# Silu of a convolution branch as z times 1/(1+exp(-z)): exponential on ACT, sum, reciprocal and product on VectorE

## What is computed

```python
def conformer_branch(z, dw_w, dw_b, ln_g, ln_b):
    a, g = jnp.split(z, 2, axis=-1)
    u = a * jax.nn.sigmoid(g)
    u = depthwise_conv(u, dw_w) + dw_b
    u = layernorm(u, ln_g, ln_b)
    return jax.nn.silu(u)
...
    merged = jnp.concatenate([
        rmsnorm(attn, g_branch[:MLA_WIDTH]),
        rmsnorm(conf, g_branch[MLA_WIDTH:MLA_WIDTH + CONF_WIDTH]),
        rmsnorm(sc, g_branch[MLA_WIDTH + CONF_WIDTH:])], axis=-1)
    return merged @ w_o
```

## Time and profile before

| | us |
|---|---|
| median of 3 runs (1690.57, 1695.78, 1696.7) | 1695.78 |
| the profiled execution, whole | 1697.5 |
| its span, first to last instruction | 1695.6 |
| TensorE matmul busy | 1610.2 |
| VectorE busy | 1026.9 |
| ACT busy | 838.2 |
| GpSimd busy | 76.3 |
| mean granted TensorE clock | 0.983 |

### The profile page before, as it was taken

One profiled execution on the slowest core, in us unless ns is written; L12 is line 12 of the kernel. 1 busy time (PEld: TensorE's weight loads), 2 busy tenths in 40 slices (PEclk: granted clock), 3 DMA queues, 4 the chain that ended last, 5 costly groups with the idle time before them and its releaser, 6 DMA issues.

```text
span 1695.6 us, 25551 instructions
## 1 busy us (share of the span) xinstructions
PE 1610.2 (95%) x10226; PEld 1379.8 (81%) x10226; DVE 1026.9 (61%) x1616; ACT 838.2 (49%) x1484; POOL 76.3 (4%) x60
## 2 busy tenths in 40 slices
PE   7998999999999999999989999999999988889997
PEld 6887789998888999987557588888888874779996
DVE  6855865567686566779764643333333687565665
ACT  5434275553826566353574552415244455665554
POOL 1200300000030000000000000000000100010000
PEclk9999999999999999999999999999999998999999
DMA  8733765556756555533101532232322231135551
GB/s 302 267 117 129 258 228 183 186 177 222 273 174 224 177 185 185 198 137 109 41 1 63 211 102 98 94 102 90 99 93 82 75 137 38 63 125 174 186 186 49
DMA packets 69937, 247.49 MB, mean 146 GB/s; under 512 B 7504, under 2 KB 10576, under 8 KB 69712
## 3 DMA queue, kind: packets, MB, share of 16 engines
q1 hardware_dynamic: 69840, 246.18, 42.4%
HBM read 245.10 MB, written 1.05 MB: 145 GB/s over the span
## 4 chain that ended last, share of the span: by engine, by line
PE 75%; DVE 12%; issue 7%; ACT 4%; DMA 0%; POOL 0%; DVEq 0%; SPq 0%; ACTq 0%; POOLq 0%
PE psum L375 15%; PE psum L377 15%; PE psum L376 14%; PE psum L396 9%; PE psum L397 5%; DVE lo_ring L336 3%; PE psum L1142 2%; PE psum L1815 2%; PE psum L410 1%; DVE c_conf L2093 1%; PE psum L411 1%; PE psum L412 1%; PE psum L1838 1%; PE psum L1825 1%; PE psum L510 1%
## 5 line engine op out<-in xcount | busy, mean ns | idle before, releaser
L375 PE MATMUL psum<-x_parts,hi_ring 128*128 128x256 f32 (+1 forms) x1464 | 459.9, 314 | 14.2 <-DVE x_parts L901 11.7
L336 DVE TENSOR_TENSOR lo_ring<-raw_ring,hi_ring 128x1024 fp32r<-128x1024 f32 x348 | 432.2, 1243 | 62.7 <-PE psum L377 21.1
L376 PE MATMUL psum<-x_parts,hi_ring 128*128 128x256 f32 (+1 forms) x1464 | 455.4, 311 | 0.0
L377 PE MATMUL psum<-x_parts,lo_ring 128*128 128x256 f32 (+1 forms) x1464 | 455.4, 311 | 0.0
L348 ACT ACTIVATE hi_ring<-raw_ring 128x1024 fp32r<-128x1024 f32 x292 | 307.3, 1053 | 256.4 <-PE psum L377 137.7
L375 PEld LDWEIGHTS psum<-x_parts,hi_ring 128*128 128x128 f32 x1464 | 280.5, 192 | 36.0 <-issue 17.6
L376 PEld LDWEIGHTS psum<-x_parts,hi_ring 128*128 128x128 f32 x1464 | 280.6, 192 | 15.0 <-issue 0.2
L377 PEld LDWEIGHTS psum<-x_parts,lo_ring 128*128 128x128 f32 x1464 | 280.5, 192 | 14.7
L396 PE MATMUL psum<-hid_parts,hi_ring 128*128 128x512 f32 x672 | 235.2, 394 | 0.3 <-DVE lo_ring L336 0.3
L1420 DVE TENSOR_TENSOR hid_parts<-relu,hid_parts 128x256 fp32r<-128x256 f32 (+1 forms) x128 | 63.0, 493 | 221.1 <-ACT relu L1409 221.1
L397 PE MATMUL psum<-hid_parts,lo_ring 128*128 128x256 f32 x672 | 188.3, 280 | 0.0
(11 more groups left out here) (430 smaller groups left out, 2344.7 us busy)
## 6 DMA issues: line engine op xcount, KB each, us to landing
raw_ring<-weights SPq DMA_DIRECT2D x460, 512.0 KB, 3.4
h_const<-hyb_consts SPq DMA_DIRECT2D x1, 1088.0 KB, 11.3
x<-xT SPq DMA_DIRECT2D x1, 1024.0 KB, 8.2
x<-ctxT SPq DMA_DIRECT2D x1, 1024.0 KB, 16.7
outT<-x SPq DMA_DIRECT2D x4, 256.0 KB, 2.5
shared<-shared_consts SPq DMA_DIRECT2D x1, 398.0 KB, 13.4
par<-params SPq DMA_DIRECT2D x1, 301.5 KB, 8.2
```

Source lines behind the costliest of these rows:

```text
L336: nc.vector.tensor_tensor(lo_ring[:, s, :], raw_ring[:, UNIT_AT[u] % RAW_SLOTS, :], hi_ring[:, s, :].bitcast(F32), ALU.subtract).then_inc( ...
L375: nc.tensor.matmul(bank(u % BANKS, T), w_hi, hi[:, k, 0:T], start=(k == 0), stop=False)
L376: nc.tensor.matmul(bank(u % BANKS, T), w_hi, lo[:, k, 0:T], start=False, stop=False)
L377: last = nc.tensor.matmul(bank(u % BANKS, T), w_lo, hi[:, k, 0:T], start=False, stop=(k == KT - 1))
```

## The change

ACT no longer computes silu. VectorE applies gain and offset itself, ACT takes exp(-z) for both halves in one instruction (the attention's table has exp), VectorE adds one, takes the reciprocal and multiplies, and ACT squares the result in one instruction. One flag, conf_gate, counts the three handovers. The new VectorE step "gate" stands at turn 6 of layer 0 and turn 5 of layer 1. Some steps after it move by a turn. In the first-block and second-block MLP the flag half_added is replaced by VectorE's own step counter; the instructions between stay.

```diff
@@ mlp_dve
-                    nc.vector.tensor_tensor(y[:, j, 0:T], side_by_side(u)[:, 0], y[:, j, 0:T], ALU.add).then_inc(flag("half_added"), 1)
+                    nc.vector.tensor_tensor(y[:, j, 0:T], side_by_side(u)[:, 0], y[:, j, 0:T], ALU.add).then_inc(dve_step, 1)
+                    link.count += 1
                     next_lo(dve, u)
-                    now["half_added"] += 1
-                    dve.wait_ge(flag("half_added"), now["half_added"])
+                    dve.wait_ge(dve_step, link.count)
@@ tables
-    PE_STEPS = [{1: ["mean"], 3: ["sums"], 5: ["sc"], 7: ["again"]}, {0: ["mean"], 3: ["sums"], 4: ["sc"], 7: ["again"]}]
-    ACT_STEPS = [{2: ["squares"], 3: ["rstd"], 5: ["silu"], 6: ["sc_rstd"], 8: ["last"]},
-                 {2: ["squares"], 3: ["rstd"], 4: ["silu"], 6: ["sc_rstd"], 7: ["last"]}]
-    DVE_STEPS = [{1: ["center"], 4: ["scaled"], 8: ["sc"], 15: ["last"]}, {1: ["center"], 3: ["scaled"], 6: ["sc"], 8: ["last"]}]
+    PE_STEPS = [{1: ["mean"], 3: ["sums"], 5: ["sc"], 8: ["again"]}, {0: ["mean"], 3: ["sums"], 4: ["sc"], 7: ["again"]}]
+    ACT_STEPS = [{2: ["squares"], 3: ["rstd"], 5: ["exp_neg"], 6: ["sc_rstd"], 7: ["squares_again"], 9: ["last"]},
+                 {2: ["squares"], 3: ["rstd"], 4: ["exp_neg"], 6: ["squares_again", "sc_rstd"], 7: ["last"]}]
+    DVE_STEPS = [{1: ["center"], 4: ["scaled"], 6: ["gate"], 8: ["sc"], 15: ["last"]}, {1: ["center"], 3: ["scaled"], 5: ["gate"], 6: ["sc"], 8: ["last"]}]
@@ branch_act
-            if step == "silu":
-                for i in range(2):
-                    act.wait_ge(flag("conf_scaled"), 2 * l + i + 1)
-                    other_set()
-                    link(nc.scalar.activation(c_conf[:, i, 0:T], c_conf[:, i, 0:T], ACT.Silu, scale=pcol("conf_g", 2 * l + i),
-                                              bias=pcol("conf_beta", 2 * l + i)))
-                    last = nc.scalar.activation(c_sq[:, i, 0:T], c_conf[:, i, 0:T], ACT.Square)
-                last.then_inc(flag("conf_sq"), 1)
+            if step == "exp_neg":
+                act.wait_ge(flag("conf_gate"), 3 * l + 1)
+                exp_set()
+                nc.scalar.activation(c_sq[:, :, 0:T], c_conf[:, :, 0:T], ACT.Exp, scale=-1.0).then_inc(flag("conf_gate"), 1)
+            if step == "squares_again":
+                act.wait_ge(flag("conf_gate"), 3 * l + 3)
+                nc.scalar.activation(c_sq[:, :, 0:T], c_conf[:, :, 0:T], ACT.Square).then_inc(flag("conf_sq"), 1)
@@ branch_dve
             if step == "scaled":
                 dve.wait_ge(flag("branch_rstd"), 2 * l + 1)
+                link(nc.vector.tensor_tensor(c_conf[:, :, 0:T], c_conf[:, :, 0:T], bc(rstd[:, 0:T], 2), ALU.mult))
                 for i in range(2):
-                    nc.vector.tensor_tensor(c_conf[:, i, 0:T], c_conf[:, i, 0:T], rstd[:, 0:T], ALU.mult).then_inc(flag("conf_scaled"), 1)
+                    last = nc.vector.tensor_scalar(c_conf[:, i, 0:T], c_conf[:, i, 0:T], pcol("conf_g", 2 * l + i), pcol("conf_beta", 2 * l + i),
+                                                   ALU.mult, ALU.add)
+                last.then_inc(flag("conf_gate"), 1)
+            if step == "gate":
+                dve.wait_ge(flag("conf_gate"), 3 * l + 2)
+                link(nc.vector.tensor_scalar(c_sq[:, :, 0:T], c_sq[:, :, 0:T], 1.0, None, ALU.add))
+                link(nc.vector.reciprocal(c_sq[:, :, 0:T], c_sq[:, :, 0:T]))
+                nc.vector.tensor_tensor(c_conf[:, :, 0:T], c_conf[:, :, 0:T], c_sq[:, :, 0:T], ALU.mult).then_inc(flag("conf_gate"), 1)
```

More of the change, by code:

```diff
@@ L1394, in late_scaled_dve @@
         lo(KT - 1)
-    now["half_added"] = 0
     def mlp_act(act, link, m, base, T):
```

## The result

| | before | after |
|---|---|---|
| median of 14 runs each, us | 1695.14 | 1701.09 |
| lowest to highest | 1690.54 to 1698.74 | 1697.38 to 1704.15 |
| span of the profiled execution | 1695.6 | 1699.7 |

The ratio is 1.0034, with a 95% interval of 1.0024 to 1.0043: the change costs 5.8 us of 1695. The forecast was 1705.6 us in a range of 1698 to 1710: the sign and the places were right, the size was too large.

What follows compares the result with a forecast made beforehand. The prediction took TensorE, waiting for ACT's silu and table loads in the attention, to bound the kernel. Layer 0's +6.0 us and layer 1's +3.8 us made +9.8 us on the median 1695.78 us: 1705.6 us, range 1698 to 1710 us.

Steps and rivals of the forecast that it cites:

- What bounds: Both layers' attention: TensorE waits behind ACT's silu and table loads; after the change the chain goes through the gate.
- about 10 us: Silu step in both layers: the time of the whole kernel said to hang on it, about 10 us.
- The loads: ACT around silu: four table loads at 1.28 us, 5.1 us in all, against 10.6 us by the skill's figure.
- The reciprocal: VectorE's gate: 8.2 us in layer 0 and 4.15 us in layer 1, called what decides.
- the floor that I supposed: 2-column reciprocal row: may rest on a minimum time, putting the slope at 8.3 ns a column, 8.7 and 4.4 us.
- The clock: TensorE behind its wait for the gate: half clock adds 2.1 us in each layer.
- The rival without a loss: TensorE behind the gates: clock isn't lost or returns at once, +5.6 us, 1701.4 us; chance 0.11.
- "scaled" hidden: VectorE: about 1 us more in layer 0 and 0.6 in layer 1, covered because top(7) waits for TensorE anyway.
- Its own range: Whole kernel: +8.1 to +11.8 us, from the ends of reciprocal and clock.
- The counter: MLP: another counter round the same instructions costs nothing, unless the wait falls differently.
- The quick reciprocal: VectorE's gate: reciprocal at one column per cycle, sum -4.9 us, 1690.9 us; chance 0.10.
- "same": Whole kernel: outcome not told from no change, within about 0.5%, 8.5 us; chance 0.44.

Runs made afterwards that it cites:

- e8: The kernel before with silu replaced by the identity, so no table is loaded for it; 1687.4 us, ratio 0.9958.
- e6: The kernel before with 8 reciprocals and 8 additions of 2 to 1024 columns added behind VectorE's last work; one run, 1708.09 us.
- e5: The changed kernel with 7 useless matmuls in each of TensorE's two waits for the gate; 1698.64 us, ratio 1.0025.
- e7: The kernel before with only the MLP's counter exchanged for VectorE's own step counter; 1696.37 us, ratio 1.0017.
- e11: A repeat of e7, the kernel before with only the MLP's counter exchanged; 1694.87 us, ratio 1.0003.
- e1: The changed kernel with the reciprocal replaced by a minimum with 1.0 of the same shape; 1688.18 us, ratio 0.996.
- e2: The changed kernel with the reciprocal dropped and the sigmoid made on ACT as exp(-ln(1+exp(-z))), VectorE keeping the product; 1689.8 us, ratio 0.9969.
- e9: The e2 kernel with layer 0's three ACT instructions at turns 5, 6 and 7 and the steps around them moved; 1689.75 us, ratio 0.9978.
- e10: A repeat of e2, beside e9 on the same chip; 1690.63 us, ratio 0.9975.

## Why the prediction was right, and where its size was off

- **What bounds.** Right: the chain left ACT, as said, and went over the gate in both layers. e8 shows that the four loads, 5.1 us long, had cost 6.9. That "about 10 us" hang on the whole step wasn't tried: no run took silu's own work out too.
- **The loads.** 1.28 us each with the next instruction at once, and 1.41 us of ACT's time by e8. By the Trainium skill's 2.66 us a switch ("ScalarE: Activation LUTs", What ACT_TABLE_LOAD costs) e8 would have gained 10.6 us, an estimate from that page, and e8's interval ends at 9.7. Here the measurement decides against that figure as a cost on this path.
- **The reciprocal.** The deciding step named rightly, and mis-sized: I took 8.2 and 4.15 us, the rows have 6.55 and 3.35, below even my lower bound of 7.7 and 3.9. I drew a line through 2 and 8 columns and carried it to 1024. The 2-column reciprocal (160 ns in the earlier trace rows, 156 in e6) lies under the line of e6 (153 + 12.5 = 165), so the slope came out at 7.3 instead of 6.25; the floor that I supposed points the wrong way, for it isn't there. The Trainium skill's repeat count of 8 ("VectorE: DVE Perf Modes", First, the fixed hardware budget), read as 8 cycles a column, isn't what e6 shows: six. That is 1.65 us of layer 0's error and 0.8 of layer 1's.
- **The clock.** Taken at 2.1 us more in each layer; e5 shows 1.6 and 1.6. I had 4 to 5.4 us of work at half clock, but part of the low stretch fell into the wait, and TensorE worked only 3.3 us in it each time. The window of 1425 to 1430 us that I leaned on the earlier trace rows was misread: in before the clock is at 0.50 from about 1417.2 to 1430.8 us, from the end of an earlier wait of 2.62 us on, and not from the wait of 2.27 us at 1425 us. The rival without a loss is out: both windows behind the gates are at 0.50. In layer 0 before had paid for its own fall as well, which the sum had in it.
- **"scaled" hidden.** True in layer 0. In layer 1, out_pair(2) waits 0.30 us for pair_out(1) behind it (the row at 1444.17 us above), and top(7) comes 0.37 us later than in before. I had looked at top(7) alone and not at pair_out(1), which stands next in VectorE's stream.
- **The sum by its own steps with measured sizes** (reciprocal, clock, and in layer 1 the overlooked wait): layer 0 is 3.9 - 1.65 + 1.6 = 3.85 (A: 3.80); layer 1 is 1.7 - 0.8 + 1.6 + 0.4 = 2.9 (B: 2.91). Forecast 6.0 and 3.8. Its own range of 8.1 to 11.8 us missed the 5.8; the wide one held it, because it had been stretched for the clock rival and the scatter. That the 1701.1 us lies on that rival's 1701.4 is luck: its mechanism is refuted, and the time came there by a shorter reciprocal (2.45 us) and a cheaper fall (1.0 us).
- **The counter** at nothing: the profiles of e7 and e11 agree, and e11's runs don't contradict it.
- **The quick reciprocal** that would have made it faster: refuted by its rows, but its direction was sound: with a short instruction in its place (e1) the kernel is 6.8 us below before by the runs and 3.6 by the stretches, where 4.9 had been reckoned.
- **Chances.** Slower by over 0.5% had 0.54 and didn't come; 0.34% lies within the 0.44 of "same", though it is clear of no change over 14 runs.

## What to carry to other kernels

Before moving a function off ACT to save a table, look for its form in the functions of the table that is in: ln and exp together made the sigmoid for 3.2 us of ACT without a load and without a slow operation elsewhere. An instruction of several us in the stream of an engine that hands small things to others can hold those others up for nearly its whole length (6.48 us of wait behind 6.55 here), and in this kernel eight pieces of it cost as much, since that engine had little spare time. List everything that stands behind a lengthened step in its stream, not the next item alone.

## What was not expected of the hardware

The reciprocal takes six cycles a column over the whole range of 8 to 1024 columns, 153 ns + 6.25 ns each (e6), where a product takes 1.04 ns and an addition with a constant 0.52 ns a column.

After the same wait of 2.7 us in the same code the clock did three different things. The window of e7 behind the wait, layer 0's attention as before:

```profile
865.50:869.50 4.00, 3.92 (x17) 2.42 (x18) 2.81 (x9) 3.97 (x9) 0.00 (x0) 1.00 0.00 0
```

And of e6:

```profile
864.75:871.00 6.25, 6.25 (x16) 4.23 (x17) 3.01 (x9) 4.92 (x12) 0.00 (x0) 0.50 0.01 3
```

In e7 it didn't fall, in before it was 0.50 for 3 us, in e6 for more than 6. A is 31.45 us in e7, 32.71 in before, 32.80 in e11, 34.10 in e6: 2.7 us between profiles with the same instructions there. The other way round, e1's 1.72 and 0.70 us close together went with a fall, and the 1.72 us alone in e2 and e8 didn't. A fall of the clock is thus a cost with a scatter of its own, and it seems that taking waits away narrows it: e2, e8 and e9 have 1.00 there, and e2's and e10's A are 30.01 and 30.02.
